# One layer of a hybrid streaming encoder on one core: the last norm's modulation product moved from TensorE to VectorE, over the feed-forward

## The reference, cut to what matters

```python
c_act = silu(c)
mod = (c_act @ ada_w + ada_b)          # 1024 x 6144: sh1 sc1 gt1 sh2 sc2 gt2
hn = rmsnorm(x, norm1_g) * (1 + sc1) + sh1
y  = token_mixer(hn, ...)              # w_in, two mixers, w_a_out, w_b_out, w_o
x  = x + gt1 * y
hn = rmsnorm(x, norm2_g) * (1 + sc2) + sh2
x  = x + gt2 * (square(relu(hn @ w_ff1)) @ w_ff2)      # d_ff = 4096
modf = (c_act @ final_ada_w + final_ada_b)             # 1024 x 2048: shf scf
y  = rmsnorm(x, final_norm_g) * (1 + scf) + shf        # the output
```

## Time and profile before

| | us |
|---|---|
| median of 3 runs | 1252.98 (1252.93 to 1253.11) |
| the profiled execution | 1251.88 |
| its span | 1250.2 |
| PE busy | 1225.0, 98% of the span |
| DVE busy | 670.6, 54% |
| ACT busy | 449.1, 36% |
| POOL busy | 117.2, 9% |
| granted clock of TensorE, mean | 0.992 of full speed |

### The profile page before, as it was taken

The page is one execution under the profiler, slowest core; times in us unless marked ns, Lnnn a source line. Parts: engine busy times, 40 slices in busy tenths (PEclk is TensorE's granted clock), DMA queues, the critical chain, the costliest instruction groups (busy, mean ns, idle before and its releaser), DMA issues.

```text
span 1250.2 us, 27424 instructions
## 1 busy us (share of the span) xinstructions
PE 1225.0 (98%) x11560; PEld 1175.0 (94%) x11560; DVE 670.6 (54%) x904; ACT 449.1 (36%) x798; POOL 117.2 (9%) x255
## 2 busy tenths in 40 slices
PE   6999999999999999999999999999999999999997
PEld 4899999999999999999999999979999999999997
DVE  5586566455464555544967984464543343343334
ACT  4584434223232222324343333363332332232254
POOL 5021111201102011011110001000300000000000
PEclk8999999999999999999999999999999999999999
DMA  9932233212222122144864567422422322222212
GB/s 274 269 89 78 76 86 94 61 52 69 62 68 63 52 84 57 35 111 153 239 199 133 158 207 287 142 61 84 129 75 84 85 85 85 84 83 76 79 52 77
DMA packets 193886, 135.44 MB, mean 108 GB/s; under 512 B 4570, under 2 KB 185276, under 8 KB 192504
## 3 DMA queue, kind: packets, MB, share of 16 engines
q1 hardware_dynamic: 186320, 105.30, 30.0%
q0 software_dynamic: 7008, 28.48, 6.8%
q10 hardware_dynamic: 456, 0.16, 0.1%
HBM read 128.02 MB, written 5.90 MB: 107 GB/s over the span
## 4 chain that ended last, share of the span: by engine, by line
PE 93%; DVE 2%; SPq 2%; ACT 2%; DMA 1%; issue 0%; DVEq 0%; ACTq 0%
PE gp L575 79%; PE dp L779 2%; PE gp L601 2%; PE dp L788 1%; SPq L308 1%; PE dp L844 1%; PE dp L810 1%; PE dp L829 1%; PE dp L837 1%; PE dp L789 1%; PE dp L749 1%; PE dp L816 1%; DMA ada_w<-in_ada_w 1%; SPq L304 1%; PE dp L819 0%
## 5 line engine op out<-in xcount | busy, mean ns | idle before, releaser
L575 PE MATMUL gp<-a_hi,w_hi 128*128 128x288 f32 x1856 | 406.9, 301 | 2.3 <-DVE w_lo L1429 2.3
L575 PE MATMUL gp<-a_hi,w_lo 128*128 128x288 f32 x1856 | 397.3, 296 | 0.0
L575 PE MATMUL gp<-a_lo,w_hi 128*128 128x288 f32 x1856 | 396.9, 295 | 0.0
L575 PEld LDWEIGHTS gp<-a_hi,w_hi 128*128 128x128 f32 x1856 | 296.8, 189 | 13.1 <-issue 4.1
L575 PEld LDWEIGHTS gp<-a_hi,w_lo 128*128 128x128 f32 x1856 | 298.8, 189 | 0.0
L575 PEld LDWEIGHTS gp<-a_lo,w_hi 128*128 128x128 f32 x1856 | 298.3, 188 | 0.0
L1429 DVE TENSOR_TENSOR w_lo<-w_raw,w_hi 128x1024 fp32r<-128x1024 f32 x160 | 196.0, 1225 | 110.3 <-ACT w_hi L1023 109.3
L1184 ACT ACTIVATE xp<-gp 128x576 f32<-128x576 f32 x113 | 73.7, 652 | 452.5 <-PE gp L575 432.4
L1023 ACT ACTIVATE w_hi<-w_raw 128x1024 fp32r<-128x1024 f32 x160 | 168.8, 1055 | 2.3 <-DMA w_raw<-in_w_in 2.2
L575 PE MATMUL gp<-f_hi,w_hi 128*128 128x288 f32 x496 | 106.8, 297 | 0.0
L575 PE MATMUL gp<-f_lo,w_hi 128*128 128x288 f32 x496 | 106.2, 296 | 0.0
(11 more groups left out here) (314 smaller groups left out, 1258.0 us busy)
## 6 DMA issues: line engine op xcount, KB each, us to landing
w_raw<-in_w_in SPq DMA_DIRECT2D x72, 512.0 KB, 3.8
w_raw<-in_w_ff SPq DMA_DIRECT2D x64, 512.0 KB, 4.0
ada_half<-in_ada_w POOLq DMA_DIRECT2D x32, 512.0 KB, 4.6
ada_w<-in_ada_w SPq DMA_DIRECT2D x16, 512.0 KB, 7.5
w_raw<-in_w_a_out SPq DMA_DIRECT2D x8, 512.0 KB, 4.4
w_raw<-in_w_b_out SPq DMA_DIRECT2D x8, 512.0 KB, 4.1
w_raw<-in_w_o SPq DMA_DIRECT2D x8, 512.0 KB, 5.8
fin_vu<-in_final_ada_w POOLq DMA_DIRECT2D x4, 1024.0 KB, 18.6
```

Of the source, the lines that this page charges most:

```text
L575: last = T_.matmul(gp[:, 2 * b + h, 0:HALF], wp[:, b, k, :], ap[:, k, h * HALF:(h + 1) * HALF], start=(k == 0 and wp is w_hi and ap is hi) ...
```

## The change

The product for the last norm is made as those of parts 1 and 2 are. In the feed-forward, DVE does one `ada_part` (one half row block for one group, 128 x 1024) behind each tile of `ff1(1)`, `ff2(0)`, `ff1(2)` and `ff2(1)`: 32 in all. PE then does `ada_reduce(3)` after `ff1(3)`, in place of all eight `ada_late`. The copy to rows, the turning and the `columns` and `scale_of` on DVE follow in and behind `ff2(2)`, where before they stood in the first quarter. POOL loads 16 halves in place of eight whole blocks, the first of them once the second norm has been made. The tile loops of DVE in the feed-forward, and of PE in `ff2(2)`, are written out. Two buffers and a semaphore fall away.

```diff
...
@@ -515,20 +509,14 @@
         pool.dma_start(t_out["s_s"][0, 0].rearrange("h k v -> k h v"), st[:, :, :]).then_inc(S["s_out"], 16)
 
         pool.wait_ge(S["o_free"], NCH + 1)
-        for m in range(4 * KT):
+        for m in range(6 * KT):
             r, k, c = 1 + m // (2 * KT), m // 2 % KT, m % 2 * D
             if m >= AS:
                 pool.wait_ge(S["ada_added"], 2 * (m - AS + 1))
-            pool.dma_start(ada_half[:, m % AS, :], ada_v[:, k, 2 * D * r + c:2 * D * r + c + D])\
-                .then_inc(late_full[m % AS], 16)
-        pool.wait_ge(S["ada_used"], 2 * KT)
-        for k in range(FIN0):
-            pool.dma_start(ada_w[:, k, :], fin_v[:, k, :]).then_inc(late_full[k], 16)
-
-        pool.wait_ge(S["tile_done"], N_WO)
-        pool.wait_ge(S["tmp_free"], 2 + 2 * KT)
-        for k in range(FIN0, KT):
-            pool.dma_start(fin_w(k), fin_v[:, k, :]).then_inc(S["fin_full"], 16)
+            if m == 4 * KT:
+                pool.wait_ge(S["h_ready"], 2 * KT)
+            src = ada_v[:, k, 2 * D * r + c:2 * D * r + c + D] if r < 3 else fin_v[:, k, c:c + D]
+            pool.dma_start(ada_half[:, m % AS, :], src).then_inc(late_full[m % AS], 16)
 
         pool.wait_ge(S["ada_row_sb"], 8)
         for e in range(2):
...
@@ -881,22 +869,6 @@
                                      start=(g == 0), stop=(g == 1))
             last.then_inc(S["ada_used"], KT)
 
-        def ada_late(k):
-
-            if k == 0:
-                pe.wait_ge(S["ada_row_sb"], 7)
-            if k < FIN0:
-                pe.wait_ge(late_full[k], 16 * ((4 * KT - k + AS - 1) // AS + 1))
-                w = ada_w[:, k, :]
-            else:
-                pe.wait_ge(S["fin_full"], 16 * (KT - FIN0))
-                w = fin_w(k)
-            for j in range(4):
-                last = T_.matmul(B2[32 * j:32 * j + 2, :], c_act[:, k, :], w[:, 512 * j:512 * j + 512],
-                                 start=(k == 0), stop=(k == KT - 1))
-            last.then_inc(S["ada_used"], 1)
-
-
         for n in range(N_TAIL + 4, N_WA):
             products(n, n % 2, a_hi, a_lo, freed="h_free" if n == N_WA - 1 else None)
             if n == N_WA - 3:
...
@@ -909,8 +881,6 @@
             pe.wait_ge(S["added"], (m + 1) * (KT - 2))
             for b in range(2):
                 if b:
-                    if m == 0:
-                        ada_late(0)
                     pe.wait_ge(S["squared"], (m + 1) * KT)
                 for h, bank in enumerate((B0, B1)):
                     last = T_.matmul(bank[:, 0:HALF], ones[:, :], acc[:, b, h * HALF:(h + 1) * HALF],
...
@@ -931,17 +901,18 @@
             if n == N_WO + 1:
                 ada_columns(B3, mrow_l, 6)
         total(0)
-        for k in range(1, KT - 1):
-            ada_late(k)
         two_products(N_FF, a_hi, a_lo, "h_ready", KT, lag=0)
-        ada_late(KT - 1)
         for k in range(2, KT):
             products(N_FF + k, k % 2, a_hi, a_lo)
         for q in range(3):
             group8(N_FF + 8 + 16 * q, a_hi, a_lo)
-            if q == 0:
+            if q < 2:
+                group8(N_FF + 16 + 16 * q, f_hi[q % 2], f_lo[q % 2], "f_split", KT * q)
+        ada_reduce(3)
+        for k in range(KT):
+            products(N_ALL - 16 + k, k % 2, f_hi[0], f_lo[0], "f_split", 2 * KT)
+            if k == 1:
                 ada_columns(B3, mrow_l, 8)
-            group8(N_FF + 16 + 16 * q, f_hi[q % 2], f_lo[q % 2], "f_split", KT * q)
         def to_tokens(f):
 
             pe.wait_ge(S["x_scaled"], f + 1)
...
@@ -1358,9 +1329,10 @@
                     free(n, n0 // 4 + i, j)
 
         ff1(0, N_FF)
-        ada_rows(B2, mrow_l, 3 * KT, 3)
         for q in range(3):
             ff1(q + 1, N_FF + 8 + 16 * q)
+            if q == 2:
+                ada_rows(B2, mrow_l, 3 * KT, 3)
             ff2(q, N_FF + 16 + 16 * q)
         for g in range(2):
             nt = (WB - 1) * NQKV + (WA - 1) * KT
...
@@ -1764,19 +1736,22 @@
         lo_split(N_TAIL + 5, 1)
         V_.memset(B2, 0.0).then_inc(S["ada_row_sb"], 1)
 
-        def ada_piece(m):
+        def ada_part(m, g):
 
             k, c = m // 2 % KT, m % 2 * D
             dve.wait_ge(late_full[m % AS], 16 * (m // AS + 1))
-            if m == 2 * KT:
-                dve.wait_ge(S["ada_used"], KT)
+            if m in (2 * KT, 4 * KT):
+                dve.wait_ge(S["ada_used"], m // 2)
+            out, w = ada_sum[:, g, c:c + D], ada_half[:, m % AS, :]
+            if k == 0:
+                TS_(out, w, c_act[:, k, g:g + 1], None, ALU.mult).then_inc(S["ada_added"], 1)
+            else:
+                dve.wait_ge(S["ada_added"], 2 * m + g - 3)
+                STT(out, w, c_act[:, k, g:g + 1], out, ALU.mult, ALU.add).then_inc(S["ada_added"], 1)
+
+        def ada_piece(m):
             for g in range(2):
-                out, w = ada_sum[:, g, c:c + D], ada_half[:, m % AS, :]
-                if k == 0:
-                    TS_(out, w, c_act[:, k, g:g + 1], None, ALU.mult).then_inc(S["ada_added"], 1)
-                else:
-                    dve.wait_ge(S["ada_added"], 2 * m + g - 3)
-                    STT(out, w, c_act[:, k, g:g + 1], out, ALU.mult, ALU.add).then_inc(S["ada_added"], 1)
+                ada_part(m, g)
 
         for t in range(KT):
             lo_split(N_TAIL + 4 + t + 2, (t + 2) % 4)
...
@@ -1860,15 +1835,16 @@
         norm(rstd2, 1)
 
         def ff1(q, n0):
-            with dve.Fori(0, 2) as i:
-                for j in range(4):
-                    n, b, t = n0 + 4 * i + j, j % 2, 4 * i + j
-                    dve.wait_ge(S["bank_free"], n + 1 + 2)
-                    STT(acc[:, b, 0:T], xp[:, b, 0:T], 0.0, xp[:, b, 0:T], ALU.max, ALU.mult).then_inc(S["tmp_free"], 1)
-                    lo_split(n + 2, (j + 2) % 4)
-                    dve.wait_ge(S["f_hi_done"], KT * q + t + 1)
-                    TT(f_lo[q % 2][:, t, :], acc[:, b, 0:T], f_hi[q % 2][:, t, :].bitcast(F32), ALU.subtract)\
-                        .then_inc(S["f_split"], 1)
+            for t in range(KT):
+                n, b = n0 + t, t % 2
+                dve.wait_ge(S["bank_free"], n + 1 + 2)
+                STT(acc[:, b, 0:T], xp[:, b, 0:T], 0.0, xp[:, b, 0:T], ALU.max, ALU.mult).then_inc(S["tmp_free"], 1)
+                lo_split(n + 2, (t + 2) % 4)
+                dve.wait_ge(S["f_hi_done"], KT * q + t + 1)
+                TT(f_lo[q % 2][:, t, :], acc[:, b, 0:T], f_hi[q % 2][:, t, :].bitcast(F32), ALU.subtract)\
+                    .then_inc(S["f_split"], 1)
+                if 1 <= q <= 2:
+                    ada_part(4 * KT + KT * (q - 1) + t // 2, t % 2)
 
         def add_residual(t, b):
             for g, c in GR:
...
@@ -1879,20 +1855,21 @@
             return mod[:, 2, ds(t + KT, 1), g] if not isinstance(t, int) else mod[:, 2, t + KT:t + KT + 1, g]
 
         def ff2(q, n0):
-            with dve.Fori(0, 2) as i:
-                for j in range(4):
-                    n, b, t = n0 + 4 * i + j, j % 2, 4 * i + j
-                    dve.wait_ge(S["bank_free"], n + 1 + 2)
-                    add_residual(t, b).then_inc(S["tmp_free"], 1)
-                    lo_split(n + 2, (j + 2) % 4)
+            for t in range(KT):
+                n, b = n0 + t, t % 2
+                dve.wait_ge(S["bank_free"], n + 1 + 2)
+                add_residual(t, b).then_inc(S["tmp_free"], 1)
+                lo_split(n + 2, (t + 2) % 4)
+                if q < 2:
+                    ada_part(4 * KT + KT * q + KT // 2 + t // 2, t % 2)
 
         ff1(0, N_FF)
         for q in range(3):
             ff1(q + 1, N_FF + 8 + 16 * q)
-            if q == 0:
+            ff2(q, N_FF + 16 + 16 * q)
+            if q == 2:
                 ch.link(columns(3, B3, "final_b", 0))
                 scale_of(2, 3, KT, "final_g").then_inc(S["mod_done"], 1)
-            ff2(q, N_FF + 16 + 16 * q)
         for t in range(KT - 1):
             n, b = N_ALL - KT + t, t % 2
             dve.wait_ge(S["bank_free"], n + 1 + 2)
```

More of the change, by code:

```diff
@@ L195, in build @@
     st = sb("st", [P, H, P], at=r_ds + 27648)
-    AS, FIN0 = 3, 3
-    ada_w = sb("ada_w", [P, AS, 2 * D], at=r_ds)
+    AS = 3
     ada_sum = sb("ada_sum", [P, 2, 2 * D], at=r_ds)
     ada_half = sb("ada_half", [P, AS, D], at=r_ds + 16384)
-    fin_vu = sb("fin_vu", [P, 4, 2 * D], at=r_v)
-    fin_k = sb("fin_k", [P, 2 * D], at=r_k)
     og = [sb("og_0", [P, T], at=r_rows), sb("og_1", [P, T], at=r_ds + 29184)]
@@ L236, in build @@
             "dve_own act_own pool_own",
-            "h_free fin_full vecs_t vecs_done xt_ready xt_done ss_all rcol_done diag1_done rb_done ab0_row ada0_t mod_f cexp_done rstd_done t_done hi_split h_ready c_act "
+            "h_free vecs_t vecs_done xt_ready xt_done ss_all rcol_done diag1_done rb_done ab0_row ada0_t mod_f cexp_done rstd_done t_done hi_split h_ready c_act "
             "ada0_used ada_row_sb ada_t mod_done ada_used ada_added ab_hi_done ab_split ab_ready row_a row_v "
@@ L277, in build @@
```

(2 more changed lines are left out.)

## The result

The changed kernel takes 1262.89 us (median of 11 runs, 1255.55 to 1264.74), the kernel before 1252.98 us (11 runs, 1251.38 to 1253.38). The medians are 9.9 us apart. The ratio worked out over the runs is 1.0073, with a 95% interval of 1.0061 to 1.0085, so the changed kernel is slower. The forecast was 1262.6 us, with a range of 1257.0 to 1267.0.

The account below looks back on a forecast made before the run. PE, 98% busy, was taken to bound the dense stretches, ACT and DVE the second norm; 1251.88 + 1.83 + 3.64 + 4.2 = 1261.55 us, with 1.1 us from profiled execution to median 1262.6 us, range 1257.0 to 1267.0.

Parts of the forecast that it names:

- Removal, gain 0: Second norm on PE: dropping eight `ada_late`, some 7.4 us, saves 0 because other engines end each wait.
- `ada_reduce(3)`, +1.83: PE, between two dense tiles: eight added matmuls cost 1.83 us, as the same piece did for part 2.
- DVE and POOL, 0: Feed-forward tiles: 32 `ada_part` of 1.28 us, 41 us on DVE, and POOL's additions are hidden, cost 0.
- The new wait, 3.64: Start of the tail: PE stands still for `mod_done` 3, set behind `ff2(2)`'s last tile, +3.64 us (3.4 to 3.9).
- The clock, 4.2 in all (1.6, 0.8, 1.8): Low clock after PE's gaps at the norm, behind `two_products` and at the tail's start: 4.2 us, 0 to about 8.
- The middle term: Gap of about 2.4 us behind `two_products`: half a chance of a short clock fall, 0.8 us.
- The sum: Whole kernel: 1251.88 + 1.83 + 3.64 + 4.2 = 1261.55 us, and 1262.6 us as median of the runs.
- The page's rule: PE idle gaps between matmul bursts bring the half-rate clock; each of the two long gaps costs a fall.
- The scatter: Runs of the changed kernel may scatter by a microsecond or two, against 0.2 us before, if low-clock lengths vary.

Follow-up runs that it names:

- when all else is mended: Changed kernel with unread matmuls around the second norm and in the tail, `columns` and `scale_of` behind `ff2(2)`'s fourth tile: 1254.76 us beside 1252.82.
- the kernel before with the step moved: Kernel before with only DVE's `columns` and `scale_of` moved behind `ff2(2)`, `ada_late` kept: 1259.05 us beside 1253.06.
- the norm filled alone: Changed kernel plus six groups of four unread matmuls behind the second norm's sums of squares: 1262.36 us.
- the DVE work left out: Changed kernel without the 32 `ada_part` on DVE and the 16 loads: 1262.37 us.
- the early scales: Changed kernel with DVE's `columns` and `scale_of` behind the fourth tile of `ff2(2)`, not the eighth: 1257.91 us.
- all three stretches filled: Changed kernel plus unread matmuls behind the sums of squares (six groups), behind `two_products` (one) and ahead of the `mod_done` wait (three): 1259.94 us.
- the norm filled and the scales early: Changed kernel, unread matmuls behind sums of squares and `two_products`, `columns`/`scale_of` after `ff2(2)`'s fourth tile: 1256.07 us; plus one group between the sums: 1256.05 us.

## Why the prediction was right

- *Removal, gain 0.* Right. The start of `two_products` moved from 820.96 to 821.03 us, and the distance from `two_products` to the next tile is 3.01 us in both. The kernel without six `ada_late` shows it alone.
- *`ada_reduce(3)`, +1.83.* Right in the piece itself, 1.83 us in the chain, but the tiles behind it take 0.2 us more (12.97 us where 12.79 is usual), which the term left out. The 1.9 us that remain when all else is mended agree with 2.0.
- *DVE and POOL, 0.* Right: the dense piece is 296.16 us with the work and 296.18 without. DVE's busy time rose by 38 us and not 41, mostly since the first four of the 32 pieces only multiply and take 0.75 us, not 1.28. In a tile of `ff1` DVE's idle time shrank from the 3.56 us of the earlier trace rows to 2.36, as one row of the changed kernel's timeline shows:

```profile
1007.55 0.76 DVE L1841 SCALAR_TENSOR_TENSOR acc<-xp 128x576 f32<-128x576 f32 x1 [2.36 <-ACT xp L1155]
```

- *The new wait, 3.64.* Measured 3.53, because the written-out loop is about 0.2 us earlier with its residual, as the range allowed: DVE's last split starts 1.74 us after PE's last matmul, where in the loop of before it was 1.91, and in the kernel before with the step moved the wait is 3.7. These are the rows that answer to the earlier trace rows:

```profile
1190.19 1.23 DVE L1401 TENSOR_TENSOR w_lo<-w_raw,w_hi 128x1024 fp32r<-128x1024 f32 x1
1191.34 0.18 DVE L1437 TENSOR_TENSOR mod<-dp,vecs 128x32 f32<-128x32 f32 x1
...
1191.76 0.17 DVE L1444 TENSOR_TENSOR scales<-scales,vecs 128x16 f32<-128x16 f32 x1
```

- *The clock, 4.2 in all (1.6, 0.8, 1.8).* The mechanism was right: the clock fell at all three places. The profiled execution lost 2.0, 1.5 and 1.5 us there, 5.0 in all, and 1.7 us by a fourth fall under the last 24 matmuls, for which the prediction had no term. The price of 0.45 us for a low microsecond holds: 5.4 us of it in dense work, less the 0.4 given back, make the 2.0 at the norm, where the prediction had taken 4.5 us. The middle term was mis-sized: half a chance of a fall, and it is there in three of the four traces that have this wait of 2.2 us (the changed kernel, the norm filled alone, the DVE work left out, but not the early scales).
- *The sum.* Between medians the clock's share is 9.9 - 2.0 - 3.5 = 4.4 us, beside the 4.2 forecast. That it came so close is in part luck. The lengths and places of the falls change from one execution to the next: the first two tiles of the tail took 13.87 us in one and 14.96 in another, and the fourth fall is in the traces of the changed kernel and of the early scales, but not in those with the norm filled alone or the DVE work left out. So the missing term and the low middle one seem to have been made up by executions in which a fall was absent or short; only one of the 11 runs has a trace.
- *The page's rule.* The emptied 5.5 us of PE are followed by 5.5 us at a granted clock of 0.52, and with filler in them the clock stays at 1.00. By that the rule of the Trainium skill, "TensorE: Matmul & The Clock Gate", section "Why this matters for your kernels" (no long gaps of an idle PE between bursts of matmuls), agrees with the traces here, where the trace of before alone could not show it. It does not cover all of them: by the rule the prediction counted two falls, and there was one behind the wait of 2.2 us and one in the tail, behind a stretch with PE busy for most of the time.
- *The scatter.* It was expected at a microsecond or two and is larger: 1255.55 to 1264.74, with nine of the eleven runs at 1260.9 or above. Why single runs come down to 1255.6 stays unexplained. The profiled execution with all three stretches filled has no fall ahead of the end and a short start phase, and still took 1257.50 us. Nor does the record point to absent falls: the mean granted clock of the run at 1255.55 is 0.984, no higher than the 0.981 to 0.987 of the nine long ones. No trace was taken of it.
- *Left open.* Each of the two versions with the norm filled and the scales early, but no filler in the tail, has 6 of 11 runs above 1256.0 us. Of the kernel before beside them, 2.0 us lower, 2 of 21 and 0 of 15 runs lie above 1254.0. One of their two traces shows a fall under the last 24 matmuls and one shows none. Whether the fall is more frequent in them than in the kernel before, which has the same instructions at this place, the runs do not say.

## What to carry to other kernels

A busy share of 98% does not price an instruction: look for what ended the wait that follows it. Work that fills a wait set by other engines is free to keep, and taking it away can cost, since it also kept TensorE's clock up. When a step is moved to spread load, follow the semaphore that it raises: here three operations of under 0.2 us each, placed behind the last tile and waited for at the head of the next stage, cost half of the loss or more (5.0 us when undone in the changed kernel, 6.0 when moved in the kernel before), and four tiles earlier no wait for them is left.

## What the runs showed of the hardware

The clock does not need a fully idle PE to fall. In the tail of the changed kernel it fell behind the first of these two rows, in which PE was recorded busy for 2.65 of 3.40 us, with transposes, products of one column and a pause of 0.75 us:

```profile
1245.95:1249.35 3.40, 2.65 (x46) 2.35 (x45) 0.62 (x1) 2.14 (x7) 0.00 (x0) 1.00 0.02 5
1249.40:1252.70 3.30, 3.30 (x19) 3.30 (x18) 2.48 (x2) 0.39 (x1) 0.00 (x0) 0.53 0.20 82
```

With four matmuls of 384 columns and only two columns of weights in that pause the median of one version was 1.9 us above the kernel before, and 3.0 without them. At the norm six such groups of 512 columns kept the clock at 1.00 through the 5.3 us that they took. What a fall costs varies for one kernel: the same 96 matmuls at the start of the tail took 13.87, 14.89 and 14.99 us in three executions with nearly the same wait ahead (3.5 to 3.7 us), and 12.78 without a fall. In the first the low clock lasted 3.4 us and began 0.5 us before the wait ended; in the last it lasted 6.8 us and began 1.3 us before.
